# Latent attention, heads 2 to 7: the rotated query stacked as rounded value and residue in one tile, its score in two fp32r passes, and its projection moved one step ahead

## The reference, cut to what matters

```python
def mla(h, cos, sin, w_down, q_norm, w_uq, kv_norm, w_ukv, w_o):
    d = h @ w_down
    cq = rms_norm(d[..., :Q_LORA_RANK], q_norm)
    ckv = rms_norm(d[..., Q_LORA_RANK:Q_LORA_RANK + KV_LORA_RANK], kv_norm)
    k_rope = apply_rope(d[..., Q_LORA_RANK + KV_LORA_RANK:], cos, sin)
    q = (cq @ w_uq).reshape(B, S, N_HEADS, QK_HEAD_DIM)
    q_rope = apply_rope(q[..., QK_NOPE_DIM:], cos[:, :, None], sin[:, :, None])
    ...
    o = causal_attention(q, k, v)
    return o.reshape(B, S, N_HEADS * V_HEAD_DIM) @ w_o
```

## Time and profile before

| what | value |
|---|---|
| median of 3 runs | 1299.62 us (1297.34 to 1299.71) |
| the profiled execution's own time | 1299.65 us |
| its span | 1297.9 us |
| mean granted TensorE clock | 0.997 |
| busy: PE | 1270.6 us (98%) |
| busy: DVE | 916.4 us (71%) |
| busy: ACT | 605.3 us (47%) |
| chain that ended last, by engine | PE 75%; DVE 13%; issue 4%; ACT 4%; DMA 2% |

### The profile page before, as it was taken

How to read it: one execution, slowest core, us unless ns; L and a number is a source line. 1 busy time by engine, 2 the same in 40 slices (tenths; PEclk the granted TensorE clock), 3 DMA queues, 4 the chain that set the end, 5 groups by cost and what they waited for, 6 DMA issues and landing times.

```text
span 1297.9 us, 19342 instructions
## 1 busy us (share of the span) xinstructions
PE 1270.6 (98%) x7379; PEld 1109.1 (85%) x7379; DVE 916.4 (71%) x1217; ACT 605.3 (47%) x881; POOL 29.3 (2%) x29
## 2 busy tenths in 40 slices
PE   7999999999999999999999999999999999999997
PEld 7779999988888777788999998888888888888876
DVE  6897787874447766579788787454768388887554
ACT  6445454553334655444454455434323255666434
POOL 0510000000000000000000000000000000000000
PEclk9999999999999999999999999999999999999999
DMA  5322424332332111231332423223624221113311
GB/s 194 109 87 66 129 67 127 90 113 89 107 103 79 30 64 66 65 97 54 109 108 86 129 87 115 90 89 106 183 65 163 66 64 34 50 49 130 98 65 66
DMA packets 156963, 119.70 MB, mean 92 GB/s; under 512 B 15132, under 2 KB 153832, under 8 KB 156648
## 3 DMA queue, kind: packets, MB, share of 16 engines
q1 hardware_dynamic: 156848, 118.89, 29.9%
q10 hardware_dynamic: 56, 0.01, 0.0%
HBM read 114.70 MB, written 4.19 MB: 92 GB/s over the span
## 4 chain that ended last, share of the span: by engine, by line
PE 75%; DVE 13%; issue 4%; ACT 4%; DMA 2%; SPq 1%; DVEq 0%; ACTq 0%
PE psum L2338 22%; PE psum L2340 22%; PE psum L2339 22%; DMA w_raw<-in_ffn_w_up 2%; PE psum L2563 1%; PE psum L2586 1%; DVE w_lo L1596 1%; DVE w_lo L1409 1%; ACT w_hi L908 1%; PE psum L2748 1%; PE psum L2720 1%; ACT w_hi L802 1%; PE psum L2732 1%; DVE second_sum L1583 1%; DVE ffn_f L1551 1%
## 5 line engine op out<-in xcount | busy, mean ns | idle before, releaser
L2338 PE MATMUL psum<-terms_hi,w_hi 128*128 128x256 f32 x952 | 270.9, 285 | 3.0 <-DVE work L1607 2.6
L2339 PE MATMUL psum<-terms_lo,w_hi 128*128 128x256 f32 x952 | 270.1, 284 | 0.0
L2340 PE MATMUL psum<-terms_hi,w_lo 128*128 128x256 f32 x952 | 270.1, 284 | 0.0
L2338 PE MATMUL psum<-xg_hi,w_hi 128*128 128x512 f32 x544 | 220.8, 406 | 3.5 <-DVE squares L1536 1.9
L2340 PE MATMUL psum<-xg_hi,w_lo 128*128 128x512 f32 x544 | 212.3, 390 | 0.0
L2339 PE MATMUL psum<-xg_lo,w_hi 128*128 128x512 f32 x544 | 212.1, 390 | 0.0
L2338 PEld LDWEIGHTS psum<-terms_hi,w_hi 128*128 128x128 f32 x952 | 183.4, 193 | 4.5 <-DVE w_lo L1596 2.8
L2339 PEld LDWEIGHTS psum<-terms_lo,w_hi 128*128 128x128 f32 x952 | 183.4, 193 | 0.1
L2340 PEld LDWEIGHTS psum<-terms_hi,w_lo 128*128 128x128 f32 x952 | 183.4, 193 | 0.0
L2338 PE MATMUL psum<-act_hi,w_hi 128*128 128x512 f32 x352 | 137.2, 390 | 0.0
L2340 PE MATMUL psum<-act_hi,w_lo 128*128 128x512 f32 x352 | 136.9, 389 | 0.0
(11 more groups left out here) (404 smaller groups left out, 2201.2 us busy)
## 6 DMA issues: line engine op xcount, KB each, us to landing
w_raw<-in_ffn_w_gate SPq DMA_DIRECT2D x68, 256.0 KB, 3.4
w_raw<-in_ffn_w_up SPq DMA_DIRECT2D x68, 256.0 KB, 3.9
w_raw<-in_w_in SPq DMA_DIRECT2D x16, 1024.0 KB, 5.4
w_raw<-in_ffn_w_down SPq DMA_DIRECT2D x16, 768.0 KB, 4.5
w_raw<-in_ffn_w_down SPq DMA_DIRECT2D x16, 640.0 KB, 4.3
w_raw<-in_ffn_w_gate SPq DMA_DIRECT2D x5, 1024.0 KB, 5.1
w_raw<-in_ffn_w_up SPq DMA_DIRECT2D x5, 1024.0 KB, 5.2
w_raw<-in_mla_w_o SPq DMA_DIRECT2D x4, 1024.0 KB, 5.0
```

What stands on the lines that cost most here:

```text
L2338: pe.matmul(o, wh, xh, start=start, stop=False, skip_group_check=True)
L2339: pe.matmul(o, wh, xl, start=False, stop=False, skip_group_check=True)
L2340: return pe.matmul(o, wl, xh, start=False, stop=stop, skip_group_check=True)
```

## The change

Pair 0 (heads 0 and 1) stays as it was. For pairs 1 to 3:

- DVE forms the rotated query itself, in `squares`: u times cos (one 128x512 product), u times sin with the two halves of 32 rows swapped (four 32x512 products, `rope_swap`), and their difference (`rope_sum`). ACT writes its rounded value to 64 rows of a free tile of `xg_hi` (two 64x512 copies, `rope_hi`), and DVE the residue to the other 64 rows (`rope_lo`, two 64x512).
- The key is stacked once: `kr_st[:, 0]` is the rounded key in both halves (two copies of ACT in step 1), `kr_st[:, 1]` its residue in both halves (two of DVE in step 2).
- The rotary score is two fp32r matmuls with the same stacked query, in place of one fp32 matmul.
- u of pairs 2 and 3 is made in the last step of an even head (steps 11 and 19) and no longer in the first of the odd one (12 and 20), and vb goes the other way; u of pair 1 stays in step 3. In head 1, qn0 and kn0 go one step later (from 4 and 5 to 5 and 6). `split_hi` of the `heads` units goes two steps sooner (6 and 14, before 8 and 16), their `split_lo` one step sooner.
- u's bank is released (`proj_released`) after the first five of the eight increments of `rope_turned`: the cos product and the four swaps.

```diff
-        q_rope = sb("q_rope", [P, 2, 2, T], stack=mla_mem)
+        q_rope = sb("q_rope", [P, 2, T], stack=mla_mem)
+        kr_st = sb("kr_st", [P, 2, T], F32R, mla_mem)
...
             if h % 2 == 0:
                 if h == 0:
                     return ((1, "u"),) if ii == 3 else ()
+                if ii == 3 and h + 2 < HEADS:
+                    return ((pr + 1, "u"),)
                 return ((pr, ("qn1", "kn1", "va", "vb")[ii]),)
-            if h == 1:
-                return ((1, ("qn0", "kn0")[ii]),) if ii < 2 else ()
-            return ((pr + 1, ("u", "qn0", "kn0")[ii]),) if ii < 3 and h + 1 < HEADS else ()
+            if h + 1 == HEADS or ii == 3 or h == 1 and ii == 0:
+                return ()
+            return ((pr, "vb") if ii == 0 else (pr + 1, ("qn0", "kn0")[ii - 1]),)
...
         def proj_released(x):
+            if x[1] == "u":
+                return sem("rope_turned"), 8 * x[0] + (1 if x[0] else 4)
...
+        def rope_pairs(s, later):
+            return [pr for pr in range(1, HEADS // 2) if s - later == NB * (2 * pr - 1) - 1]
+        def rope_tiles(pr, e):
+            x = xg_hi[:, QR + 2 * (pr % 2) + e, :]
+            return (x[64 * e:64 * e + 64, :], x[64 - 64 * e:128 - 64 * e, :], x)
...
                 for s in range(NB * HEADS + 3):
                     h, ii = divmod(s, NB)
+                    for pr in rope_pairs(s, 3):
+                        act.wait_ge(sem("rope_turned"), 8 * pr + 2)
+                        act.activation(rope_tiles(pr, 0)[0], squares[0:64, 0, :], ACT.Copy)
+                        act.activation(rope_tiles(pr, 1)[0], squares[64:128, 0, :], ACT.Copy).then_inc(*mark(f"rope_hi{pr}"))
...
-                    if h % 2 == 0 and ii == 0 and 0 < h < HEADS:
-                        split_hi(FIRST["heads"] + 1 + h // 2)
+                    if s == 1:
+                        act.activation(kr_st[0:64, 0, :], kr[0:64, :], ACT.Copy)
+                        act.activation(kr_st[64:128, 0, :], kr[0:64, :], ACT.Copy).then_inc(*mark("kr_st"))
+                    if h % 2 == 1 and ii == 2 and h + 3 < HEADS:
+                        split_hi(FIRST["heads"] + 1 + (h + 1) // 2)
+                    if s == NB * (HEADS - 2):
+                        split_hi(FIRST["mla_o"])
...
+                def rope_swap(pr, e):
+                    ps = proj_result(PROJ_ORDER.index((pr, "u")))
+                    for r0, r1 in ((64 * e, 64 * e + 32), (64 * e + 32, 64 * e)):
+                        dve.tensor_tensor(squares[r0:r0 + 32, 1, :], ps[r1:r1 + 32, :], sin_t[r1:r1 + 32, :], ALU.mult).then_inc(sem("rope_turned"), 1)
+                def rope_sum(pr):
+                    dve.wait_ge(sem("rope_turned"), 8 * pr + 1)
+                    dve.tensor_tensor(squares[:, 0, :], squares[:, 0, :], squares[:, 1, :], ALU.subtract).then_inc(sem("rope_turned"), 1)
+                def rope_lo(pr):
+                    dve.wait_ge(*at(f"rope_hi{pr}"))
+                    for e in range(2):
+                        hi, lo, _ = rope_tiles(pr, e)
+                        dve.tensor_tensor(lo, squares[64 * e:64 * e + 64, 0, :], hi.bitcast(F32), ALU.subtract).then_inc(sem("rope_turned"), 1)
...
                 for s in range(NB * HEADS + 1):
                     h, ii = divmod(s, NB)
+                    for pr in rope_pairs(s, 1):
+                        proj(pr, "u")
+                    for pr in rope_pairs(s, 2):
+                        rope_swap(pr, 1)
                     if s < NB * HEADS:
                         row_max(s)
...
                     if s:
                         normalise(s - 1)
+                    for pr in rope_pairs(s, 2):
+                        rope_sum(pr)
+                    for pr in rope_pairs(s, 3):
+                        rope_lo(pr)
+                    if s == 2:
+                        dve.wait_ge(*at("kr_st"))
+                        for r in range(0, P, 64):
+                            low = dve.tensor_tensor(kr_st[r:r + 64, 1, :], kr[0:64, :], kr_st[0:64, 0, :].bitcast(F32), ALU.subtract)
+                        low.then_inc(*mark("kr_lo"))
...
                     if h < 2:
                         pe.matmul(o, q_rope[:, hs, q], kr[:, k], start=False, stop=False, skip_group_check=True)
+                    else:
+                        turned_q = rope_tiles(h // 2, hs)[2][:, q]
+                        pe.matmul(o, turned_q, kr_st[:, 0, k], start=False, stop=False, skip_group_check=True)
+                        pe.matmul(o, turned_q, kr_st[:, 1, k], start=False, stop=False, skip_group_check=True)
```

More of the change, by code:

```diff
@@ L440, in program @@
         for pr in range(4):
-            used[FIRST["heads"] + pr] = (sem("proj_done"), 7 * pr + 7)
+            used[FIRST["heads"] + pr] = (sem("proj_done"), 7 * pr + 7 + (pr in (1, 2)))
             used[FIRST["mla_o"] + pr] = (sem("mla_o_done"), 2 * pr + 2)
@@ L1806, in proj @@
                     done = sem("proj_ready")
-                    if idx:
-                        dve.wait_ge(done, RESIDUED.index((pr, what)))
                     if what == "u":
@@ L1811, in proj @@
                         ps = proj_result(idx)
+                        if pr:
+                            dve.tensor_tensor(squares[:, 0, :], ps[:, :], cos_t[:, :], ALU.mult).then_inc(sem("rope_turned"), 1)
+                            rope_swap(pr, 0)
+                            return
                         for e in range(2):
                             r = slice(64 * e, 64 * e + 64)
-                            dve.tensor_tensor(q_rope[0:64, pr % 2, e, :], ps[r, :], cos_t[r, :], ALU.mult).then_inc(sem("rope_turned"), 1)
-                            sine = dve.tensor_tensor(q_rope[64:128, pr % 2, e, :], ps[r, :], sin_t[r, :], ALU.mult)
-                            sine.then_inc(*((done, 1) if e else (sem("rope_turned"), 1)))
+                            dve.tensor_tensor(q_rope[0:64, e, :], ps[r, :], cos_t[r, :], ALU.mult).then_inc(sem("rope_turned"), 1)
+                            dve.tensor_tensor(q_rope[64:128, e, :], ps[r, :], sin_t[r, :], ALU.mult).then_inc(sem("rope_turned"), 1)
                         return
-                    hi = [x for x in RESIDUED if x[1] != "u"].index((pr, what)) + 1
-                    dve.wait_ge(sem("proj_hi"), hi)
+                    n = RESIDUED.index((pr, what))
+                    if n:
+                        dve.wait_ge(done, n)
+                    dve.wait_ge(sem("proj_hi"), n + 1)
                     dve.tensor_tensor(proj_tiles(idx, xg_lo), proj_result(idx), proj_tiles(idx, xg_hi).bitcast(F32), ALU.subtract).then_inc(done, 1)
@@ L1859, in mla @@
                         for t in after_step(*divmod(s - 1, NB)):
-                            proj(*t)
+                            if t[1] != "u":
+                                proj(*t)
                     if s:
                         normalise(s - 1)
+                    for pr in rope_pairs(s, 2):
[7 more added lines that the diff above has]
+                        low.then_inc(*mark("kr_lo"))
                     if s - 1 in VALUE_STEPS and s % 2 == 0:
                         head_out(VALUE_STEPS[s - 1][0])
-                    if h % 2 == 0 and h and ii >= 1:
-                        split_lo(FIRST["heads"] + 1 + h // 2, ii - 1)
+                    if h % 2 == 0 and h and ii < 3 and h + 2 < HEADS:
+                        split_lo(FIRST["heads"] + 1 + h // 2, ii)
+                    if h == HEADS - 2 and ii >= 1:
+                        split_lo(FIRST["mla_o"], ii - 1)
                     if h + 1 == HEADS and ii >= 1:
```

17 lines of the change are left out of this document (10 added, 7 removed).

## The result

| | before | after |
|---|---|---|
| median, four runs each | 1299.45 us | 1309.78 us (1309.03 to 1310.75) |
| ratio | | 1.0083, 95% interval 1.0070 to 1.0096 |
| profiled execution, span | 1297.9 us | 1307.1 us |
| mean granted clock | 0.997 | 0.993 |
| busy PE, DVE, ACT | 1270.6, 916.4, 605.3 | 1270.7, 926.0, 611.6 us |

The change costs 10.3 us between the medians. 1305.5 was predicted, and the measured time is 0.8 us above the range. Slower was right; the size was not. All medians and ratios here are of fast executions; one execution of the whole record was slow (1787.72 us at a mean clock of 0.655, in the run with ACT's order altered) and isn't counted.

The account below looks back on a forecast made before the run. PE was taken as the bound, held at pair borders by DVE's queue from u to kn0's residue. 4.0 + 0.95 + 0.85 - 1.2 + 1.3 = +5.9 us on 1299.65 gave 1305.5 us, eight-in-ten range 1300.5 to 1309.

Parts of the forecast that it names:

- Step 8, +4.0: First border of pairs: DVE's longer queue to kn0's residue makes PE stand 4.8 us; step 8 begins 4.0 us later.
- Steps 16 and 24, +0.95 and +0.85: Later borders: PE waits 2.2 us before qn0 in steps 13 and 21; step 16 begins 0.95 us later, step 24 0.85.
- The end, -1.2: Heads 6 and 7, nothing added: PE keeps 0.83 us of head 6 and 0.37 of step 28.
- The clock, +1.3: Behind step 8's stand: half rate for 2.6 us loses 1.3 us of work, counted once; bounds 0 and 3.9.
- clock falls again and again: Rival, chance 0.10: the clock falls also at qn0 in steps 13 and 21, giving 1308.1 us.
- DMA, +0: Weight unit that step 6 now rounds: loaded 13 us before step 0, so DMA costs nothing.
- hidden by 0.2 us: Before step 8: ACT's 1.48 us weight unit delays kn0's copy to 443.8; DVE comes at 444.0, so no cost.
- Faster: Rival, chance 0.09: DVE's 9.7 us fit into its 20.7 us of waits, PE never stands at borders: 1293.2 to 1296 us.

Follow-up runs that it names:

- kept warm: The changed kernel plus matmuls without use where PE stands (18 at the end of step 7, 7 before qn0 in steps 13 and 21): 1303.85 us, 1.0030.
- the order alone: The kernel before with only the change's order of u, vb, qn0, kn0 and weight units, its arithmetic as before: 1306.38 us, 1.0050.

## Why the prediction was wrong in size and right in kind

- **Step 8, +4.0.** Measured +4.51. PE stood 5.10 us where 4.8 was walked. The sum ended at 439.84, qn0's copy at 441.76 and kn0's residue at 445.52 (predicted 439.2, 440.95, 444.7, with this execution's step 0 itself 0.38 later). Of the excess of 0.44, 0.26 was there when the sum ended, and the rest is ACT: its 64x512 copies go at 0.64 us, not 0.54. Right.
- **Steps 16 and 24, +0.95 and +0.85.** Without the clock's part they are +1.22 and +1.25 (25.83 - 24.61, 25.83 - 24.58). The wait before qn0 was taken as 2.2 and was 2.22. Right to 0.4 us, but partly by luck: the terms listed from step 12 to step 16 (5.3, 0.25, 2.14 for qn0 as for u, 0.7 and 4.2 on DVE) add up to 12.6 us and not to the 13.1 that was used; kept warm, the stretch took 13.41.
- **The end, -1.2.** Measured -0.88 - 0.39 = -1.27. The gain on PE, 0.83 a head, shows as 0.88 between steps 24 and 28.
- **The clock, +1.3: this is the step that failed.** It was counted once. It fell three times and cost 4.0 us in the traces (kept warm) and 5.9 between the medians, so the count was wrong and not the price: three falls at 1.3 are 3.9. The rival "clock falls again and again" (0.10) was the mechanism, and its 1308.1 lacks only the 1.1 us by which the borders were longer. The error of the sum is 9.69 - 5.9 = 3.8 us, of which 2.7 is this term. The prediction held 2.2 us of standing to be safe and called the fall at the program's end the trace's only one. It was not. PE's timeline before, and a window there:

```profile
120.32 0.36 PE L2338 MATMUL psum<-terms_hi,w_hi 128*128 128x256 f32 x1 [2.43 <-DVE work L1607]
...
121.73 0.42 PE L2340 MATMUL psum<-terms_hi,w_lo 128*128 128x256 f32 x1
...
121.00:122.00 1.00, 1.00 (x10) 1.00 (x9) 1.00 (x2) 0.00 (x0) 0.00 (x0) 0.83 0.00 0
```

After a wait of 2.43 us the clock fell at 121.7, 1.3 us after PE had resumed, for 3.4 us (a matmul of 256 lasts 0.42 in place of 0.28): the very pattern of steps 13 and 21, in the kernel before.
- **DMA, +0.** Right: no wait of ACT for a weight unit appears.
- **The weight unit "hidden by 0.2 us".** Right in the change, but the order alone shows the cover: once DVE is on time it costs 1.06 us.
- **Faster (0.09).** It asked for 4.8 us of queue to vanish. Taking that work off the way, and not off DVE, made the kernel faster than before, by 3.1 us with all three pairs and six idle matmuls (0.9977) and by 3.6 with two pairs (0.9975); the 1296 at most that this rival named was not reached.

The rule of the Trainium skill that the prediction weighed ("TensorE: Matmul & The Clock Gate", section "Why this matters for your kernels": no idle gaps over about 3 us) would have had the clock stay up in the waits of 2.22 us. The measurement decides against it here: both were followed by a fall.

What stays open: what the clock's fall costs in a median to better than 1 us, since it doesn't come in every execution (4.0 us by the traces and 5.9 by the medians for three falls), and why a wait of about 2 us brings one at one time and not at another.

## What to carry to other kernels

Busy time says how much an engine could take on, not where. Follow the queue from the new work to the instruction that the bound engine waits for, and put ahead of that instruction only what its consumer needs first; the same work behind it was nearly free (10.3 us slower became level with before, 0.9997, by moves alone, and 3.1 us faster with six idle matmuls and one more move). An edit that only moves a wait has found a symptom; try it again once the queue is short. And look for a fall of the clock behind each stand of about 2 us or more, not behind the longest alone; more than half of those of 1.8 to 2.7 us had one here.
